# Two layers of a hybrid streaming encoder on one core: the order of scores, values and dense products in the local attention

## The reference, cut to what matters

```python
s = jnp.einsum('bnqhd,bnkhd->bhnqk', q, kb) * (LA_HD ** -0.5)
s = jnp.where(valid, s + bias, NEG_INF)
p = jax.nn.softmax(s, axis=-1)
o = jnp.einsum('bhnqk,bnkhd->bnqhd', p, vb)
```

## Time and profile before

| | |
|---|---|
| median of 3 runs | 3390.66 us (3390.39 to 3394.1) |
| profiled execution, its own time | 3392.02 us |
| its span, first to last instruction | 3390.2 us |
| mean granted TensorE clock | 0.969 |
| busy: PE, PEld | 3187.3 us (94%), 2557.0 us (75%) |
| busy: DVE, ACT, POOL | 1561.4 us (46%), 726.5 us (21%), 1758.2 us (52%) |

### The profile page before, as it was taken

The page is one execution under the profiler, slowest core; times in us unless marked ns, Lnnn a source line. Parts: engine busy times, 40 slices in busy tenths (PEclk is TensorE's granted clock), DMA queues, the critical chain, the costliest instruction groups (busy, mean ns, idle before and its releaser), DMA issues.

```text
span 3390.2 us, 42235 instructions
## 1 busy us (share of the span) xinstructions
PE 3187.3 (94%) x14648; PEld 2557.0 (75%) x14648; DVE 1561.4 (46%) x1950; ACT 726.5 (21%) x1293; POOL 1758.2 (52%) x1003
## 2 busy tenths in 40 slices
PE   6999998889999899999999999988999998999997
PEld 5888765578887767888778887656888887778885
DVE  3332445765545535332343323558555464443323
ACT  1110113422221222111021102233222212221101
POOL 5666552333346654666656664424333557456662
PEclk9999999999999998999999999998999999999998
DMA  3222221111122222323222232212111223222231
GB/s 133 97 95 100 84 87 38 56 57 50 51 81 87 90 85 66 104 96 99 99 77 98 96 103 84 69 38 69 50 56 51 87 87 107 72 78 93 99 99 50
DMA packets 78864, 272.62 MB, mean 80 GB/s; under 512 B 8176, under 2 KB 12560, under 8 KB 78736
## 3 DMA queue, kind: packets, MB, share of 16 engines
q1 hardware_dynamic: 73504, 264.27, 23.5%
q10 hardware_dynamic: 5088, 5.96, 0.6%
q0 software_dynamic: 144, 0.66, 0.0%
HBM read 268.73 MB, written 2.12 MB: 80 GB/s over the span
## 4 chain that ended last, share of the span: by engine, by line
PE 81%; DVE 8%; issue 6%; POOL 2%; ACT 1%; DMA 0%; DVEq 0%; POOLq 0%; ACTq 0%; SPq 0%
PE acc L544 71%; PE aux L544 9%; POOL wl L529 1%; DVE dc L1633 1%; POOL wh L527 1%; DVE xl L1500 1%; DVE tmp L1688 1%; PE aux L707 1%; DVE dc L1631 1%; DVE xf L1555 0%; DMA raw<-in_stream 0%; ACT tmp L1134 0%; DVE sc L1595 0%; DVE sc L1609 0%; DVE lc L1694 0%
## 5 line engine op out<-in xcount | busy, mean ns | idle before, releaser
L527 POOL TENSOR_SCALAR wh<-raw 128x1024 fp32r<-128x1024 f32 x496 | 537.7, 1084 | 1541.7 <-PE acc L544 778.8
L529 POOL TENSOR_TENSOR wl<-raw,wh 128x1024 fp32r<-128x1024 f32 x496 | 1221.2, 2462 | 41.4
L544 PE MATMUL acc<-xh,wh 128*128 128x512 f32 x2432 | 995.8, 409 | 80.6 <-POOL wl L529 36.7
L544 PE MATMUL acc<-xh,wl 128*128 128x512 f32 x2432 | 963.7, 396 | 0.0
L544 PE MATMUL acc<-xl,wh 128*128 128x512 f32 x2432 | 963.5, 396 | 0.0
L544 PEld LDWEIGHTS acc<-xh,wh 128*128 128x128 f32 x2432 | 465.6, 191 | 215.7 <-issue 70.1
L544 PEld LDWEIGHTS acc<-xh,wl 128*128 128x128 f32 x2432 | 465.9, 192 | 100.9
L544 PEld LDWEIGHTS acc<-xl,wh 128*128 128x128 f32 x2432 | 466.9, 192 | 91.1 <-issue 2.9
L544 PE MATMUL acc<-hh,wl 128*128 128x512 f32 x704 | 278.2, 395 | 0.0
L544 PE MATMUL acc<-hh,wh 128*128 128x512 f32 x704 | 278.2, 395 | 0.0
L544 PE MATMUL acc<-hl,wh 128*128 128x512 f32 x704 | 278.2, 395 | 0.0
(11 more groups left out here) (266 smaller groups left out, 3786.1 us busy)
## 6 DMA issues: line engine op xcount, KB each, us to landing
raw<-in_stream SPq DMA_DIRECT2D x496, 512.0 KB, 3.4
xf<-in_xT SPq DMA_DIRECT2D x1, 2048.0 KB, 10.0
bias<-rel_scratch ACTq DMA_DIRECT2D x2, 1024.0 KB, 5.6
mraw<-in_memT ACTq DMA_DIRECT2D x2, 1024.0 KB, 5.0
out_xT<-xf SPq DMA_DIRECT2D x1, 2048.0 KB, 7.1
gate_w<-in_gate_w ACTq DMA_DIRECT2D x2, 512.0 KB, 3.5
const<-in_const POOLq DMA_DIRECT2D x1, 640.0 KB, 8.2
sc<-in_ba_w ACTq DMA_DIRECT2D x2, 256.0 KB, 2.6
```

Of the source, the lines that this page charges most:

```text
L527: pool.tensor_scalar(wh[:, s, :], raw[:, s, :], 1.0, 0.0, ALU.mult, ALU.add).then_inc(hi_step, 1)
L529: pool.tensor_tensor(wl[:, s, :], raw[:, s, :], wh[:, s, :].bitcast(F32), ALU.subtract).then_inc(unit_split, 1)
L544: return pe.matmul(out, w, x, start=start, stop=stop, skip_group_check=True)
```

## The change

Only the order of instructions on PE and DVE changes; counts, shapes and buffers stay. In PE's step n, `score(n + 2)` comes first rather than behind `turn(n)`. `values(h)` comes in the first step of the next head, behind that step's score, rather than at the end of its own head's last step. On DVE, `out_low` stays in steps 9, 17 and 25 and comes behind `lru_beside(n)`.

```diff
                 score(0)
                 score(1)
                 for n in range(HA * CH):
+                    if n + 2 < HA * CH:
+                        score(n + 2)
+                    if n and n % CH == 0:
+                        values(n // CH - 1)
                     lru_part(n)
                     turn(n)
-                    if n + 2 < HA * CH:
-                        score(n + 2)
-                    if n % CH == CH - 1:
-                        values(n // CH)
+                values(HA - 1)
 
                 pe.wait_ge(yc_lo.sem, yc_lo.at(l, KB))
...
                     if n >= 1:
                         normalise(n - 1)
-                    if n >= 2 and (n - 1) % (2 * CH) == 0:
-                        out_low((n - 1) // (2 * CH) - 1)
                     lru_beside(l, n)
+                    if n >= 2 * CH and n % (2 * CH) == 1:
+                        out_low(n // (2 * CH) - 1)
```

## The result

The changed kernel takes 3361.95 us (median of 4 runs, 3360.91 to 3363.27) against 3390.52 us (now 4 runs of the kernel before, 3383.37 to 3394.1), a ratio of 0.992 with a 95% interval of 0.9908 to 0.9932: 0.8% faster. The forecast was 3357, its range 3346 to 3374. The profiled execution has a span of 3359.1 us where that of before has 3390.2: 31.1 us less, 33.2 forecast.

The account below looks back on a forecast made before the run. PE, holding 81% of the chain, was taken as the bound, with waits and low clock in the attention loops. Savings of 19.2 and 14.0 us, together 33.2, took the 3390.7 median to 3357; range 3346 to 3374.

Parts of the forecast that it names:

- Scores ahead: PE in ordinary heads: score n+1 issued ahead of the products of n-1 removes the turns' waits of 0.51 and 0.73 us.
- Values a step late: PE between heads: values behind the next head's score lose their 0.14 us wait; at the loop's end 0.7 us stays.
- Low part: DVE steps 9, 17, 25: low part behind the convolution step leaves 0.83 and 0.55 us late, 1.4 us per such head.
- The main choice, no fall of the clock behind the waits that remain: Low-part heads: remaining waits of 0.83 and 0.55 us leave PE's granted clock without a fall; forecast's chance 0.66.
- Rival A: Clock still falls in heads with a low part, costing 12 to 16 us; time 3369 to 3373; chance 0.22.
- The sum: Both attention loops: 107.2 us of work and waits each; 19.2 us less in the first layer, 14.0 in the second, together 33.2.
- the second layer starts its loop at a low clock, which nothing here removes: Second layer's loop opening: clock 0.88 over 14.13 us, 1.7 us lost, taken to stay after the change.
- rival C: Clock falls after heads' values, up to 3.5 us each, 14 in all; 3373 at half, 3406 at all; chance 0.02.
- at best 10 us: Low end of the forecast's own range 3350 to 3364: all low-part-head waits and the low start go, 6 x 1.4 + 1.7.
- B: DVE's normalise 9 held by POOL's split if 0.5 us of room closes: 6 to 14 us, time 3363 to 3385; chance 0.06.
- D: Behind the loop, a weight unit or DVE's leftovers give back up to 33 us: 3384 to 3391; chance 0.04.

Follow-up runs that it names:

- Scores and values alone: Against the changed kernel: PE's new order kept, DVE's low part put back ahead of the convolution part; 3371.5 us, span 3367.6.
- Values in their own head: Against the changed kernel: each head's values put directly behind its own last turn, with no score between; 3373.03 us, span 3375.3.

## Why the prediction was right

**Scores ahead.** Right. Both waits of an ordinary head are gone, and the head takes 12.70 us where 12.79 was summed. "Scores and values alone" has the same 12.7 without the low part's move.

**Values a step late.** Right: no idle ahead of any but the last values, 0.69 us there. The margin was thin, 1.39 us of work over 1.28 of waiting. "Values in their own head" shows the 0.7 us bare, and 0.2 to 0.3 more a head that I had not counted.

**Low part.** Right in size and reason: 1.80, 0.83 and 0.55 us were forecast for the low part's end, turn 9 and turn 10; 1.86, 0.89 and, for turn 10, 0.49 (0.34 us of idle) came out (531.20 against 529.22 + 1.49 = 530.71). The third such head is shorter, 13.9 us.

**The main choice, no fall of the clock behind the waits that remain.** Right. Twelve of twelve such heads in two profiles of the changed kernel hold 1.00. Rival A, at 0.22, did not happen. The experiments show where it would have: at 1.4 us in one head of six, at 1.93 to 2.02 in three of six; the waits that remained, up to 0.73 us, stand clear of that. The ground given for the choice was weaker than it looked, since it compared with waits of 1.31 to 1.49 us in other places, and at turn 9 a wait of 1.4 us can have a fall. The rule of the Trainium skill that was set against it (TensorE: Matmul & The Clock Gate, section on psum-queue depth-cycling) speaks of short idles that come often. That does not agree with this trace: behind no idle of under 1 us between a loop's opening and its end is there a fall, with or without the change; the falls there stood behind single waits of 1.39 us and more.

**The sum.** 33.2 us forecast, 31.1 in the span, 28.6 in the medians. The term that was off is "the second layer starts its loop at a low clock, which nothing here removes", with nothing for the first: the first loop opened with 5.2 us lost in the profiled execution. The rest of the loops came out 1.6 and 1.2 us shorter than the 107.2 summed (105.6, 106.0 without the openings); heads of 12.70 us rather than 12.79, and a third low-part head without its second wait, are about 2 of these 2.8 us. 5.2 less 2.8 is 2.4 us; 33.2 - 2.4 = 30.8, the loops' gain. I had taken the first layer's 1.00 for a property of the kernel, from one execution; by the table of openings it is partly chance and perhaps partly the old order. Two errors of opposite sign made the sum look better than its terms, and so did the parts outside the loops (2.8 us less, 2.5 more), which had been taken to shift as a block.

Two numbers of the prediction do not follow from its own terms: seven falls at 3.5 us in rival C give 3357 + 24.5 = 3382 us, not 3373, and "at best 10 us" gives 3347, not the 3350 of the forecast's own range. Neither bears on what came out.

**Rivals B, C, D.** No normalise was held by a split, with the room as narrow as forecast. Nothing fell behind values. The gain was not given back: PE's first row behind the 9.1 us wait moved from 674.72 to 659.14, by the first loop's own 15.6 us.

```profile
659.14 0.77 PE L544 MATMUL acc<-ych,wh 128*128 128x512 f32 x1 [9.12 <-DVE ycl L1501]
```

## What to carry to other kernels

Where two engines hand a tile back and forth, compute the loop's latency against the work that stands between issue and need, and put the producer's order one step ahead before shortening anything. On an in-order engine, place an instruction that waits on another engine behind all work that is ready; one step later still, and its wait can vanish for everyone, as it did here. Of a clock that can fall, forecast every stretch behind a wait as a range, for one execution shows only one of the courses that it can take.

## What the runs showed of the hardware

At turns 9, 17 and 25 of this kernel the granted clock's fall behind a wait of PE looked like chance that grows with the wait: none in 18 cases under 1 us, one in six at 1.4, three in six at 2.0, six in six at 2.2. The length of the wait alone doesn't decide it: at the loop's end no fall stood behind 20 waits of 1.49 us, while at the opening a wait of 2.58 us was followed by no loss in three cases and one of 1.2 us by losses of 1.7 or 5.2 us in all four. How long the clock stays down differs for the same program in the same place: 1.7 or 5.2 us were lost at the first loop's opening in two executions of the changed kernel.

A convolution step of 128x512 on DVE that began while POOL's `wl` split ran ended 0.3 us behind the split, in the kernel before and in the changed one: it took 1.22 us rather than 0.55 where it began 1.46 us into the split, and 2.60 rather than 0.48 where it began 0.09 us into it.
